# Latent attention heads: query columns of two heads in one product, rotary rows made once, blocks scaled at the end

## Chip, cores and metric

The kernel runs on one core of a Trainium2 chip. The metric is the time of one execution on the device in microseconds, as a median over runs; the engines are called PE (TensorE), DVE (VectorE), ACT (ScalarE), POOL (GpSimd), and SP is the queue that issues the DMAs.

## What is computed

Two decoder layers over 1024 rows of width 1024. The first layer's mixer is stick-breaking attention, the second's is latent attention; both layers have four memory heads and a SwiGLU. The change touches only the latent attention of the second layer, which has 12 heads, each with 64 plain and 32 rotary query columns:

```python
q = (_rms(c_q, mla_q_norm[j]) @ mla_w_q_up[j]).reshape(b, s, N_MLA_HEADS, MLA_QK)
kv = (_rms(c_kv, mla_kv_norm[j]) @ mla_w_kv_up[j]).reshape(b, s, N_MLA_HEADS, MLA_NOPE + MLA_V)
k = jnp.concatenate([kv[..., :MLA_NOPE], k_rope_h], axis=-1)
q = _rms(q, mla_g_qn[j])
k = _rms(k, mla_g_kn[j])
q = jnp.concatenate([q[..., :MLA_NOPE], _rope(q[..., MLA_NOPE:], positions)], -1)
k = jnp.concatenate([k[..., :MLA_NOPE], _rope(k[..., MLA_NOPE:], positions)], -1)
o = _causal_softmax_attn(q.transpose(0, 2, 1, 3), k.transpose(0, 2, 1, 3), v.transpose(0, 2, 1, 3))
```

## The kernel before

`latent_heads` works through the 12 heads as six pairs. Products in full precision are made of three matmuls each (`product3`, lines 84 to 86: high by high, low by high, high by low), so every operand is split into a high part (ACT copies it) and a low part (DVE or POOL subtracts).

**Preparing a pair.** The work is cut into units, and all units of a pair share one PSUM bank (`bank`, number 7), except in the opening, which has four. A unit waits until the one before it has left the bank (`free` and `released`). The units are: `kv 0` to `kv 3`, keys and values of 256 rows each, 12 matmuls of 256 columns; `q 0` to `q 3`, queries of one head and one half of the rows (`halves`: head 0 rows 0 to 511, head 0 rows 512 to 1023, then head 1), 18 matmuls of 512 columns each. The weights of a head are widened from 96 to 128 columns: the 32 rotary columns stand there a second time with their halves swapped, and one multiplication with `rope_table` does gain and rotation in one, because the scores sum over both copies. `ss` and `rq` (one each per head) sum the squares of the queries over the 96 columns by a matmul with `ones` and turn the sums with four transposes, `qnorm` makes the inverse root from them, and `kturn 0` to `kturn 3` turn the keys.

**Attention of a pair.** A pair has four jobs in the order of `halves`. A job has four score rows (128 queries each, against 128 to 512 keys in a half 0, against 640 to 1024 in a half 1), numbered 0 to 15 in the turn, and a softmax in the rows: DVE takes the maximum (line 1212) and multiplies it by the query's inverse root (line 1217), ACT takes the exponential and the row sum (line 1181), DVE takes the inverse of the sum (line 1226, step `I`) and multiplies the row by it (line 1232, step `R`). Then come 4 or 8 blocks of 128 keys, together 24 in a turn, numbered by `tau`: PE transposes a block (step `T`, line 1153), ACT copies it as the high part (line 1193), DVE subtracts the low part (line 1237), and two blocks later PE multiplies both with the values (step `V`, lines 1165 and 1167). `T` of a block waits for the low part of two blocks earlier. After the last block of a job, step `E` copies one half of the output bank (ACT, line 1199), adds the other (DVE, line 1243) and the block goes to DRAM. There is one output bank, so the first `V` of the next job waits for that addition.

**The order** is written out by hand. Turn `g` of a hardware loop runs the attention of pair `g` and between its blocks prepares pair `g + 1`: the dictionary `extras` says behind which `tau` a unit stands, and `plan` says how many score rows are made by the end of each `tau` (it runs 9 rows ahead into the next pair, so the rows 16 to 24 of a turn belong to the next pair). The list `OPENING` prepares pair 0. There are six turns; the last, here called the closing turn, prepares nothing. SP has one queue for the loads of weights and the stores of the output blocks. After the phase, `project_and_swiglu` begins.

## Time and profile before

| | |
|---|---|
| median of 3 runs | 2628.85 us (2626.62 to 2630.59) |
| the profiled execution | 2629.66 us, its span 2627.9 us |
| PE, DVE, ACT, POOL busy | 96%, 66%, 50%, 42% of the span |
| opening of the latent heads | 1482.5 to 1526.6 us, 44.1 us |
| turns 0 to 4 | 1526.6 to 1846.0 us, 319.4 us |
| closing turn | 1846.0 to 1884.3 us, 38.3 us |

The page gives each engine's busy time as a share of the span. The stretches of the latent heads come from the timeline: the opening begins with the first matmul of `kv 0`, and turn 0 with the first transpose of a block. A line can be that of a helper, so all products stand at lines 84 to 86; the tile names tell them apart.

### The profile page before, as it was taken

What the parts mean: (1) busy time and instruction counts of PE and PEld (TensorE: products, weight loads), DVE (VectorE), ACT (ScalarE), POOL (GpSimd) and SP (SyncE); (2) the same over time, 40 slices, a digit from 0 to 9 for tenths busy, and PEclk for the clock granted to TensorE, in tenths of its full rate; (3) what the DMA queues carried; (4) which work ended last, traced back from release to release, by engine and by line L of the source; (5) the groups of instructions that cost most, each with busy time, mean ns of one, the idle gap of its engine ahead of it and who ended that gap; (6) DMA issues with size and microseconds to landing.
All of it is one profiled execution on the core that took longest, in us unless ns stands there. A gap on an engine that the chain in (4) does not pass through costs nothing. (4 is left out here: it accounts for less than half of the span.)

```text
span 2627.9 us, 37382 instructions
## 1 busy us (share of the span) xinstructions
PE 2526.2 (96%) x12150; PEld 2057.7 (78%) x12150; DVE 1739.8 (66%) x2659; ACT 1310.6 (50%) x2483; POOL 1112.5 (42%) x839
## 2 busy tenths in 40 slices
PE   7999999999999999999989999999899999999999
PEld 6867777667888888888777777778687888888887
DVE  6767787855765666478655377777648665665595
ACT  6567777745433333444655366666545333333443
POOL 2134454311465566555411332332003665565554
PEclk9999999999999999999999999999899999999999
DMA  4111110153222232674302000000242322234843
GB/s 145 45 29 33 33 33 9 33 176 113 81 100 104 100 112 88 228 240 148 107 21 59 14 20 22 21 21 21 83 166 90 116 100 104 100 112 143 285 125 117
DMA packets 182796, 242.76 MB, mean 92 GB/s; under 512 B 31376, under 2 KB 105872, under 8 KB 182672
## 3 DMA queue, kind: packets, MB, share of 16 engines
q1 hardware_dynamic: 182672, 241.19, 27.7%
q8 instruction: 68, 1.11, 0.2%
q14 instruction: 56, 0.46, 0.1%
HBM read 175.60 MB, written 65.54 MB: 92 GB/s over the span
## 5 line engine op out<-in xcount | busy, mean ns | idle before, releaser
L2385 POOL TENSOR_TENSOR l0s_run_lo<-l0s_run,l0s_run_hi 128x512 fp32r<-128x512 f32 (+2 forms) x120 | 143.5, 1195 | 215.6 <-DVE l0s_run_hi L2538 215.6
L477 POOL TENSOR_TENSOR l1f_wd_lo<-l1f_d,l1f_wd_hi 128x512 fp32r<-128x512 f32 x77 | 108.0, 1403 | 104.6 <-ACT l1f_wd_hi L552 104.6
L477 POOL TENSOR_TENSOR l0f_wd_lo<-l0f_d,l0f_wd_hi 128x512 fp32r<-128x512 f32 x77 | 109.3, 1422 | 97.2 <-ACT l0f_wd_hi L552 97.0
L84 PE MATMUL banks<-l1f_T_hi,l1f_op_hi 128*128 128x512 f32 x352 | 137.1, 390 | 1.1 <-DVE l1f_T_lo L697 1.1
L84 PE MATMUL banks<-l0f_T_hi,l0f_op_hi 128*128 128x512 f32 x352 | 137.1, 390 | 1.0 <-DVE l0f_T_lo L697 1.0
L85 PE MATMUL banks<-l0f_T_lo,l0f_op_hi 128*128 128x512 f32 x352 | 137.0, 389 | 0.0
L85 PE MATMUL banks<-l1f_T_lo,l1f_op_hi 128*128 128x512 f32 x352 | 136.9, 389 | 0.0
L86 PE MATMUL banks<-l1f_T_hi,l1f_op_lo 128*128 128x512 f32 x352 | 136.9, 389 | 0.0
L86 PE MATMUL banks<-l0f_T_hi,l0f_op_lo 128*128 128x512 f32 x352 | 136.9, 389 | 0.0
L439 POOL TENSOR_TENSOR l1f_s<-l1f_raw 128x512 f32<-128x512 f32 x44 | 66.6, 1513 | 158.1 <-DMA l1f_raw<-in_w_ffn_gu_dram 135.3
L509 ACT ACTIVATE l1f_op_hi<-l1f_s 128x512 fp32r<-128x512 f32 x88 | 55.2, 631 | 140.4 <-PE banks L86 140.4
L509 ACT ACTIVATE l0f_op_hi<-l0f_s 128x512 fp32r<-128x512 f32 x88 | 55.2, 631 | 140.4 <-PE banks L86 140.4
L462 POOL TENSOR_TENSOR l1f_hid<-l1f_c,l1f_gate 128x512 f32<-128x512 f32 x44 | 67.5, 1535 | 129.6 <-DVE l1f_c L719 129.6
L462 POOL TENSOR_TENSOR l0f_hid<-l0f_c,l0f_gate 128x512 f32<-128x512 f32 x44 | 67.0, 1524 | 129.5 <-DVE l0f_c L719 129.5
L84 PE MATMUL banks<-ht_hi,l0s_w_hi 128*128 128x512 f32 x288 | 119.6, 415 | 1.4 <-DVE l0s_q L2033 1.2
L84 PE MATMUL banks<-l0f_wd_hi,l0f_a_hi 128*128 128x512 f32 x308 | 120.0, 390 | 0.6 <-DVE l0f_a_lo L760 0.6
L439 POOL TENSOR_TENSOR l0f_s<-l0f_raw 128x512 f32<-128x512 f32 x44 | 66.5, 1512 | 127.0 <-DMA l0f_raw<-in_w_ffn_gu_dram 102.9
L1237 DVE TENSOR_TENSOR l1aa_pt_lo<-banks,l1aa_pt_hi 128x512 fp32r<-128x512 f32 (+2 forms) x144 | 78.8, 554 | 62.3 <-ACT l1aa_pt_hi L1193 61.9
L86 PE MATMUL banks<-l0f_wd_hi,l0f_a_lo 128*128 128x512 f32 x308 | 119.8, 389 | 0.0
L85 PE MATMUL banks<-l0f_wd_lo,l0f_a_hi 128*128 128x512 f32 x308 | 119.8, 389 | 0.0
L84 PE MATMUL banks<-l1f_wd_hi,l1f_a_hi 128*128 128x512 f32 x308 | 119.8, 389 | 0.0
L85 PE MATMUL banks<-l1f_wd_lo,l1f_a_hi 128*128 128x512 f32 x308 | 119.8, 389 | 0.0
(536 smaller groups left out, 8456.1 us busy)
## 6 DMA issues: line engine op xcount, KB each, us to landing
l0f_raw<-in_w_ffn_gu_dram SPq DMA_DIRECT2D x22, 1024.0 KB, 5.0
l1f_raw<-in_w_ffn_gu_dram SPq DMA_DIRECT2D x22, 1024.0 KB, 4.9
l0f_a_raw<-hidden_rows SPq DMA_DIRECT2D x77, 256.0 KB, 3.9
l1f_a_raw<-hidden_rows SPq DMA_DIRECT2D x77, 256.0 KB, 3.4
...
```

The costliest lines, as they stand in the source:

```text
L84: pe.matmul(out, l_hi, r_hi, start=first, stop=False, skip_group_check=True)
L85: pe.matmul(out, l_hi, r_lo, start=False, stop=False, skip_group_check=True)
L86: return pe.matmul(out, l_lo, r_hi, start=False, stop=last, skip_group_check=True)
L439: pool.tensor_tensor(out[:], left, right, op).then_inc(s_made, 1)
L462: pool.tensor_tensor(hidden(q), cs[q][:], gate[q][:], ALU.mult).then_inc(hid_done, 1)
L477: pool.tensor_tensor(wd_lo[g % RING][:], held[HELD_AT[DOWN[p][1]]][i][:], as_f32(wd_hi[g % RING][:]), ALU.subtract).then_inc(wd_lo_done, 1)
L509: act.activation(op_hi[n][:], stationary(n, b), ACT.Copy).then_inc(op_hi_done, 1)
L1237: dve.tensor_tensor(self.pt_lo[tau % self.np][:, c0:HALF], self.t_ps[tau % 2][:, c0:HALF], as_f32(self.pt_hi[tau % self.np][:, c0:HALF]), ...
L2385: pool.tensor_tensor(run_lo[x % NR][:, f:HALF], run[x % NR][:, f:HALF], as_f32(run_hi[x % NR][:, f:HALF]), ALU.subtract).then_inc(run_spli ...
```

## The change

The four query units of a pair become two. `q 0` and `q 1` now make only the 64 plain columns, of both heads side by side in one 128 column product, for one half of the rows each, in two parts of nine matmuls. The rotary columns of all 12 heads are made in the opening, in three groups of four heads (`rope b half`, six units of 18 matmuls), multiplied by two tables spread over the partitions, stored in DRAM (`rope_dram`), and fetched for each pair by six DMAs into the lower half of `q32`. Squares are summed by matmuls with the squares as weights and two columns of ones (`twos`, or `fours` for the rotary groups, units `rss`), which need no turning afterwards; the rotary part of the sum goes through DRAM too (`base_dram`). The exponentials are no longer multiplied by the inverse row sum: step `R` is gone, step `I` takes four sums at once, and the inverse sums go to DRAM and come back spread over 64 partitions, where a second DVE operation in step `E` multiplies the output block by them. The order in `extras` and `plan` is new.

```diff
-    OPENING = ["kv 0", "kv 1", "kv 2", "kv 3", "q 0 0", "ksum 0", "q 0 1", "q 0 2", "knorm 0", "q 1 0", "q 1 1",
-               "wk", "ksum 1", "q 1 2", "kturn 0", "ss 0", "knorm 1", "rq 0", "qnorm 0", "S", "S", "q 2 0", "q 2 1",
-               "S", "kturn 1", "wq 0", "q 2 2", "q 3 0", "S", "S", "q 3 1", "S", "q 3 2", "S", "kturn 2", "ss 1",
-               "wq 1", "rq 1", "kturn 3", "S", "v0", "qnorm 1"]
-    extras = {0: ["q 0 0", "q 0 1"], 1: ["v1", "q 0 2"], 3: ["kv 0"], 4: ["kv 1"], 5: ["kv 2", "ksum 0"],
-              6: ["kv 3", "knorm 0", "wk"], 7: ["q 1 0", "ksum 1", "q 1 1", "q 1 2", "knorm 1"], 8: ["ss 0"],
-              9: ["rq 0"], 10: ["kturn 0"], 11: ["kturn 1"], 12: ["qnorm 0", "q 2 0", "wq 0"], 13: ["q 2 1", "v0"], 15: ["q 2 2"],
-              16: ["q 3 0"], 17: ["q 3 1", "q 3 2"], 18: ["wq 1", "kturn 2"], 19: ["ss 1"],
-              20: ["rq 1", "qnorm 1"], 21: ["kturn 3"]}
-    plan = [9, 9, 9, 9, 10, 10, 11, 12, 12, 12, 13, 14, 15, 16, 17, 18, 18, 20, 20, 21, 22, 22, 23, 24, 25]
+    OPENING = ["kv 0", "kv 1", "kv 2", "kv 3", "wr 1", "rope 0 0", "ksum 0", "rope 0 1", "knorm 0", "rss 0 0", "q 0 0", "ksum 1",
+               "rss 0 1", "q 0 1", "knorm 1", "ss 0", "kturn 0", "q 1 0", "rq 0", "q 1 1", "qhi 0", "qnorm 0", "kturn 1", "ss 1",
+               "wr 2", "rope 1 0", "S", "qhi 1", "rq 1", "S", "qnorm 1", "S", "rope 1 1", "S", "rss 1 0", "kturn 2", "S", "qhi 2",
+               "rss 1 1", "S", "kturn 3", "S", "qhi 3", "S", "S", "rope 2 0", "wq", "wk", "rope 2 1", "rss 2 0", "v0", "rss 2 1"]
+    extras = {1: ["v1"], 2: ["kv 0"], 3: ["kv 1"], 4: ["kv 2", "ksum 0"], 5: ["kv 3", "knorm 0"], 6: ["q 0 0", "ksum 1", "wk"],
+              7: ["q 0 1", "knorm 1"], 8: ["ss 0", "rq 0"], 9: ["qhi 0"], 10: ["kturn 0", "qnorm 0"], 11: ["kturn 1"], 12: ["q 1 0"],
+              13: ["q 1 1", "v0"], 14: ["ss 1", "rq 1", "qhi 1"], 15: ["qhi 2", "wq"], 16: ["kturn 2", "qnorm 1"], 17: ["qhi 3"],
+              18: ["kturn 3"]}
+    plan = [9, 9, 9, 9, 10, 11, 12, 13, 13, 14, 15, 16, 16, 17, 18, 18, 19, 20, 20, 21, 22, 22, 23, 24, 25]
...
             elif kind == "I":
-                s = 4 * step[0] + step[1]
-                one = slice(s % 4, s % 4 + 1)
-                dve.wait_ge(self.exp_done, turn * self.ns + s + 1)
-                dve.reciprocal(self.rinv[:, one], self.rsum[:, one]).then_inc(self.inv_done, 1)
-            elif kind == "R":
...
-                dve.tensor_scalar(row[:], row[:], self.rinv[:, one], None, ALU.mult).then_inc(self.rows_done, 1)
+                n = step[0]
+                dve.wait_ge(self.exp_done, turn * self.ns + 4 * n + 4)
...
+                dve.reciprocal(self.rinv[n % 2][:], self.rsum[n % 2][:]).then_inc(self.inv_done, 1)
...
             elif kind == "E":
                 n = step[0]
                 dve.wait_ge(self.tmp_done, turn * self.nj + n + 1)
+                dve.tensor_tensor(self.o_sum, self.o_ps[n % len(self.o_ps)][0:HD, :], self.o_tmp, ALU.add).then_inc(self.out_done, 1)
+                dve.wait_ge(self.out_done, 1 + turn * self.nj + n + 1)
                 dve.wait_ge(self.stored[n % 2], 16 + 16 * (turn * (self.nj // 2) + n // 2))
-                dve.tensor_tensor(self.o_out[n % 2][:], self.o_ps[n % len(self.o_ps)][0:HD, :], self.o_tmp[:],
-                                  ALU.add).then_inc(self.out_done, 1)
+                dve.wait_ge(self.scale_in[n % 2], 16 * (turn * (self.nj // 2) + n // 2 + 1))
+                dve.tensor_tensor(self.o_out[n % 2], self.o_sum, self.o_scale[n % 2], ALU.mult).then_inc(self.out_scaled, 1)
...
+    def store_scale(self, sp, n, turn=0):
+        sp.wait_ge(self.inv_done, turn * self.nj + n + 1)
+        with self.nc.allow_non_contiguous_dma("row scales"):
+            sp.dma_start(self.scale_dram[n % self.nj].rearrange("(i p) -> p i", p=P), self.rinv[n % 2][:]).then_inc(self.scale_stored[n % 2], 16)
...
+                elif kind == "rope":
+                    b, half = int(n[0]), int(n[1])
+                    if half == 0:
+                        pe.wait_ge(wr_lo, b + 1)
+                    free(what, g)
+                    for c in range(NQ):
+                        last = product3(pe, bank_of(what, g)[:], wr["hi"][b % 2][:, c, :], wr["lo"][b % 2][:, c, :],
+                                        cq["hi"][:, c, columns(half)], cq["lo"][:, c, columns(half)], c == 0, c == NQ - 1)
+                    last.then_inc(rope_made, 1)
...
                 elif kind == "ss":
-                    h = int(n[0])
...
-                    for half in range(2):
-                        last = pe.matmul(bank_of(what, g)[half * HD:(half + 1) * HD, :], ones[:], q_sq[half][:],
+                    half = int(n[0])
                     free(what, g)
+                    pe.wait_ge(q_squared, 2 * g + half + 1)
+                    for i in range(HT):
+                        last = pe.matmul(bank_of(what, g)[:, 2 * i:2 * i + 2], q_sq[half][:, i * P:(i + 1) * P], twos[:],
                                          start=True, stop=True, skip_group_check=True)
```

The first place is on PE, at the start of a turn of the loop: the blocks tau 0 to 2, whose transposes read `l1aa_p` and whose products read `l1a_v`. Before, from the end of the first two parts of `q 0`:

```order
L84 MATMUL banks<-cq_hi,l1a_wq_hi_14507 128x512
L85 MATMUL banks<-cq_lo,l1a_wq_hi_14507 128x512
L86 MATMUL banks<-cq_hi,l1a_wq_lo_14509 128x512
L1153 MATMUL banks<-ident,l1aa_p_1_14536 128x128
L1153 MATMUL banks<-ident,l1aa_p_2_14537 128x128
L1153 MATMUL banks<-ident,l1aa_p_3_14538 128x128
L1165 MATMUL banks<-l1aa_pt_hi_14553,l1a_v 128x128
L1167 MATMUL banks<-l1aa_pt_lo_14556,l1a_v 128x128
L84 MATMUL banks<-cq_hi,l1a_wq_hi_14507 128x512
L85 MATMUL banks<-cq_lo,l1a_wq_hi_14507 128x512
L86 MATMUL banks<-cq_hi,l1a_wq_lo_14509 128x512
```

And in the change, from the transposes of tau 1 to the first product of the next job:

```order
L1142 MATMUL banks<-ident,l1aa_p_1_14535 128x128
L1142 MATMUL banks<-ident,l1aa_p_2_14536 128x128
L1142 MATMUL banks<-ident,l1aa_p_3_14537 128x128
L1154 MATMUL banks<-l1aa_pt_hi_14552,l1a_v 128x128
L1156 MATMUL banks<-l1aa_pt_lo_14555,l1a_v 128x128
L1140 REGISTER_ALU
L1142 MATMUL banks<-ident,l1aa_p_2_14536 128x128
L1142 MATMUL banks<-ident,l1aa_p_3_14537 128x128
L1150 ISA
L3530 ISA
L1154 MATMUL banks<-l1aa_pt_hi_14550,l1a_v 128x512
L1156 MATMUL banks<-l1aa_pt_lo_14553,l1a_v 128x512
```

The 18 matmuls of a query unit, 12 behind tau 0 and 6 behind tau 1, stand there no longer; the transposes of tau 2 follow the product of tau 1 directly.

The second place is on DVE, around the end of job 2 (tau 16 and 17). Before, from the maximum of a score row to the addition of the output block and what follows it:

```order
L1226 RECIPROCAL l1aa_rinv<-l1aa_rsum 128x1
L1232 TENSOR_SCALAR l1aa_p_1_14536<-l1aa_p_1_14536,l1aa_rinv 128x256
L1209 REGISTER_ALU
L1212 TENSOR_REDUCE l1aa_raw_nmx<-banks 128x1
L1217 TENSOR_TENSOR l1aa_nmx<-l1aa_raw_nmx,l1a_rq 128x1
L1236 REGISTER_ALU
L1237 TENSOR_TENSOR l1aa_pt_lo_14556<-banks,l1aa_pt_hi_14553 128x512
L1241 REGISTER_ALU
L1242 ISA
L1243 TENSOR_TENSOR l1aa_o_out_14562<-banks,l1aa_o_tmp 64x512
```

And in the change (`l1aa_parts` is the sum before scaling):

```order
L1203 TENSOR_REDUCE l1aa_raw_nmx<-banks 128x1
L1208 TENSOR_TENSOR l1aa_nmx<-l1aa_raw_nmx,l1a_rq 128x1
L3403 REGISTER_ALU
L3407 SCALAR_TENSOR_TENSOR l1a_kt_lo<-banks,l1a_gcol,l1a_kt_hi 128x512
L3333 TENSOR_TENSOR l1a_q_a<-l1a_q_y 128x8
L3335 SCALAR_TENSOR_TENSOR l1a_q_b<-l1a_q_a,l1a_q_dev 128x8
L3336 REGISTER_ALU
L3337 SCALAR_TENSOR_TENSOR l1a_rq<-l1a_q_b,l1a_q_y 128x8
L1222 REGISTER_ALU
L1223 TENSOR_TENSOR l1aa_pt_lo_14555<-banks,l1aa_pt_hi_14552 128x512
L1228 TENSOR_TENSOR l1aa_parts<-banks,l1aa_parts 64x512
```

The low part of `kturn 2` and the three operations of `qnorm 1` have moved ahead of the last low part and of the addition that frees the output bank; the scaling of rows is gone.

## Rows read from the trace of the kernel before

**Rows 1.** Windows: one turn (turn 2) and the closing turn.
```profile
core 0: us, PE busy (x) PEld busy (x) DVE busy (x) ACT busy (x) POOL busy (x), PEclk, DMA share, GB/s
1606.15:1670.00 63.85, 60.37 (x361) 50.43 (x360) 50.09 (x121) 42.01 (x100) 18.19 (x19) 1.00 0.08 22
1846.00:1884.30 38.30, 31.49 (x153) 25.89 (x154) 26.66 (x59) 20.65 (x43) 1.27 (x1) 0.78 0.18 55
```
**Rows 2.** Waits of PE in one turn: us in total, times, longest.
```profile
PE banks L3347 <- DVE l1a_kt_lo L3268: 1.0, 1, 1.0
...
PE banks L1165 <- DVE l1aa_o_out L1243: 0.5, 2, 0.3
```
**Rows 3.** Timeline of PE: a query unit, its 4th and last matmul, then `ss`.
```profile
1543.60 0.39 PE L84 MATMUL banks<-cq_hi,l1a_wq_hi 128*128 128x512 f32 x1
...
1546.79 0.40 PE L86 MATMUL banks<-cq_hi,l1a_wq_lo 128*128 128x512 f32 x1
...
1548.79 1.08 PE L3347 MATMUL banks<-l1a_q_sq,l1a_ones 128*64 128x512 f32 x4 [0.70 <-ACT l1a_q_sq L3161]
1549.80 0.55 PE L1153 MATMUL banks<-ident,l1aa_p 128*128 128x128 f32 x3
...
1551.74 0.62 PE L3355 MATMUL banks<-ident,l1a_q_sq 128*128 128x128 f32 x4
1552.19 0.38 PE L1153 MATMUL banks<-ident,l1aa_p 128*128 128x128 f32 x2
```
**Rows 4.** Timeline of PE: sums with two columns, phase before.
```profile
1479.11 1.95 PE L2923 MATMUL banks<-l1i_ones,l1i_q_sum 128*128 128x2 f32 x16 [0.84 <-POOL l1i_q_sum L2750]
```
**Rows 5.** Waits of PE in the opening.
```profile
PE banks L3355 <- ACT l1a_q_sq L3167: 2.5, 2, 1.8
PE banks L3347 <- ACT l1a_q_sq L3161: 1.6, 2, 1.1
```
**Rows 6.** Timeline of PE, start of turn 2, with query parts between.
```profile
1650.09 0.22 PE L2984 MATMUL banks<-causal,ident_r 128*128 128x128 f32 x1
...
1658.19 0.49 PE L1165 MATMUL banks<-l1aa_pt_hi,l1a_v 128*128 128x512 f32 x1 [0.30 <-DVE l1aa_o_out L1243]
```
**Rows 7.** Timeline of PE, start of the closing turn, nothing between.
```profile
1841.33 0.22 PE L2984 MATMUL banks<-causal,ident_r 128*128 128x128 f32 x1
...
1847.78 0.66 PE L1153 MATMUL banks<-ident,l1aa_p 128*128 128x128 f32 x2 [2.79 <-DVE l1aa_pt_lo L1237]
1848.79 0.77 PE L1165 MATMUL banks<-l1aa_pt_hi,l1a_v 128*128 128x512 f32 x1 [0.35 <-issue]
```
**Rows 8.** Timeline of DVE, same place.
```profile
1846.10 0.93 DVE L1232 TENSOR_SCALAR l1aa_p<-l1aa_p,l1aa_rinv 128x1024 f32<-128x1024 f32 x2
1846.94 1.15 DVE L1237 TENSOR_TENSOR l1aa_pt_lo<-banks,l1aa_pt_hi 128x512 fp32r<-128x512 f32 x2
1848.01 0.67 DVE L1243 TENSOR_TENSOR l1aa_o_out<-banks,l1aa_o_tmp 64x512 f32<-64x512 f32 x1
```
**Rows 9.** Windows: granted clock behind that start (columns as in rows 1).
```profile
1848.00:1850.00 2.00, 1.65 (x6) 0.98 (x6) 1.11 (x3) 0.38 (x1) 1.27 (x1) 0.50 0.07 17
...
1854.00:1856.00 2.00, 1.38 (x10) 1.17 (x10) 1.60 (x3) 1.55 (x3) 0.00 (x0) 0.97 0.68 267
...
1528.00:1530.00 2.00, 0.48 (x3) 0.05 (x1) 2.00 (x3) 0.38 (x1) 2.00 (x2) 1.00 0.00 0
```
**Rows 10.** Timeline of PE: `kturn 0` and `kturn 1`, one score row between.
```profile
1617.51 0.62 PE L3364 MATMUL banks<-ident,l1a_k 128*128 128x128 f32 x4
...
1620.44 0.63 PE L3364 MATMUL banks<-ident,l1a_k 128*128 128x128 f32 x4 [0.55 <-DVE l1a_kt_lo L3268]
```
**Rows 11.** Groups by line, whole program: count, busy us, mean ns.
```profile
L1232 DVE TENSOR_SCALAR l1aa_p<-l1aa_p,l1aa_rinv 128x128 f32<-128x128 f32 (+3 forms) x96 | 53.8, 565 | 2.3
...
L3268 DVE SCALAR_TENSOR_TENSOR l1a_kt_lo<-banks,l1a_gcol,l1a_kt_hi 128x512 fp32r<-128x512 f32 x24 | 17.9, 745 | 4.9 <-ACT l1a_kt_hi L3176 4.9
...
L1226 DVE RECIPROCAL l1aa_rinv<-l1aa_rsum 128x1 f32<-128x1 f32 x96 | 14.7, 153 | 3.3 <-ACT l1aa_p L1181 3.3
```

More of the change, by code:

```diff
@@ L1064, in __init__ @@
                           for j in range(blocks_of(half))]
-        steps, made, exps, inverses, rows = [], 0, 0, 0, 0
+        steps, made, exps = [], 0, 0
         def score_up_to(count):
@@ L1070, in score_up_to @@
                 exp_up_to(made)
-                row_up_to(made - 1)
                 steps.append(("S", made // 4, made % 4))
                 made += 1
+                if made % 4 == 1 and made > 4:
+                    steps.append(("I", made // 4 - 1))
         def exp_up_to(count):
@@ L1112, in __init__ @@
             steps += rest
-        row_up_to(plan[-1])
+        exp_up_to(plan[-1])
         self.steps = steps
         self.first_steps = [s for s in steps if s[0] not in "VE" or s[1] >= 0]
-        self.closing = [s for s in steps if s[0] not in "SPIR" or s[1] < self.nj] + (rest if wrap else [])
+        self.closing = [s for s in steps if s[0] not in "SPI" or s[1] < self.nj] + (rest if wrap else [])
     def product(self, tau):
@@ new lines, in load_base, with store_rotary, spread_table @@
+            def load_base(g):
+                sp.dma_start(base[:].rearrange("p a h i -> p (a h i)"), base_dram[:, bass.ds(g * G, G)]).then_inc(base_in, 16)
+            def store_rotary(r):
+                b, half = ROPES[r]
+                sp.wait_ge(rope_copied, r + 1)
+                for kind in range(2):
+                    sp.dma_start(rope_dram[kind, b * P:(b + 1) * P, columns(half)], rope_out[kind][r % 2][:]).then_inc(rope_stored[r % 2], 16)
+            def spread_table():
+                for n in range(4):
+                    for kind, row, first, count in ((0, HD, 0, ROPE), (1, HD + ROPE + H, 0, H), (1, HD + ROPE, H, H)):
+                        at_row = n * ROPE + first
+                        sp.dma_start(tables[kind][at_row:at_row + count, :], table[row:row + count, :]).then_inc(spread, 16)
@@ L3155, in prepare @@
                     u = int(n[0])
                     h, half = halves[u]
[L3157 to L3167 removed]
+                    act.wait_ge(rope_in[h], 48 * (g + 1))
@@ L3168, in prepare @@
+                    act.wait_ge(q_scaled[h], 2 * g + half + 1)
+                    act.activation(qt["hi"][:, h, columns(half)], q32[:, h, columns(half)], ACT.Copy).then_inc(q_hi, 1)
                 elif kind == "ksum":
@@ L3271, in ready @@
             def ready(dve, h, half, g):
-                dve.wait_ge(q_scale, 2 * g + h + 1)
+                dve.wait_ge(q_scale, 2 * g + half + 1)
             dve.memset(gcol[:], 1.0).then_inc(made_ones, 1)
-            dve.memset(ones[0:QK, :], 1.0)
-            dve.memset(ones[QK:P, :], 0.0).then_inc(made_ones, 1)
+            for h in range(2):
+                dve.memset(twos[h * HD:(h + 1) * HD, h:h + 1], 1.0)
+                dve.memset(twos[h * HD:(h + 1) * HD, 1 - h:2 - h], 0.0)
+            for i in range(4):
+                for j in range(4):
+                    last = dve.memset(fours[i * ROPE:(i + 1) * ROPE, j:j + 1], 1.0 if i == j else 0.0)
+            last.then_inc(made_ones, 1)
             at_.dve(dve, opening, 0, lambda dve, what, g: prepare(dve, what, 0), ready)
@@ L3319, in prepare @@
                         pe.wait_ge(wk_lo, g + 1)
+                        if isinstance(g, int) and g == 1:
+                            for s in range(2):
+                                pe.wait_ge(rope_stored[s], 96)
                     free(what, g)
@@ L3326, in prepare @@
                     last.then_inc(kv_made, 1)
+                elif kind == "rope":
+                    b, half = int(n[0]), int(n[1])
+                    if half == 0:
[5 more added lines that the diff above has]
+                    last.then_inc(rope_made, 1)
+                elif kind == "rss":
+                    r = 2 * int(n[0]) + int(n[1])
+                    if r == 0:
+                        pe.wait_ge(made_ones, 2)
+                    free(what, g)
+                    pe.wait_ge(rope_squared, r + 1)
+                    for i in range(HT):
+                        last = pe.matmul(bank_of(what, g)[:, 4 * i:4 * i + 4], q_sq[r % 2][:, i * P:(i + 1) * P], fours[:],
+                                         start=True, stop=True, skip_group_check=True)
+                    last.then_inc(rss_made, 1)
```

418 lines of the change are left out of this document (261 added, 157 removed).

## The prediction

> **What bounds the kernel now.** I read the windows first, cut at the borders of the phase [rows 1]. In turn 2 PE is busy 60.4 of 63.85 us at the full clock, against 50.1 for DVE, 42.0 for ACT and 18.2 for POOL. So PE bounds the turn, and what a change takes from its instructions comes back only as far as no other chain is laid bare. Next I read what PE waits for in that turn: five entries, 1.0 the longest and 0.5 the shortest [rows 2], in all 3.3 us; nearly every chain of DVE and ACT is covered. The closing turn shows the same attention without cover: PE has 31.5 us of work in 38.3, at 0.78 of the clock [rows 1]. It is the only sample of what a turn does when PE runs out of work, and it is my measure for the new one. Then I read the places where a turn is thinnest, its start and the turns of keys, and price them one by one.
>
> **PE, per turn.** From the fourth matmul of a query unit at 1543.60 to its eighteenth at 1546.79 [rows 3] there are 14 steps: 3.19 / 14 = 0.228 us each. Seventy-two matmuls become 36: 36 x 0.228 = **-8.2**. A head's `ss` holds PE for 1.01 (1548.79 to 1549.80) and its turning for 0.45 (1551.74 to 1552.19) [rows 3], together 1.46. The new `ss` of a half is eight products with two columns; sixteen such took 1.95 [rows 4], so 0.97 for eight. Two of them: **-1.0**. PE alone would give 63.85 - 9.2 = 54.7 us a turn.
>
> **DVE, ACT, POOL, SP, per turn.** DVE loses 16 row scalings of 565 ns and 12 of 16 inverses of 153 ns [rows 11]: -9.0 and -1.8. Four further multiplications of 64x512, by the addition of the same shape at 0.67 [rows 8], give +2.7. That is no term of the sum, since DVE doesn't bound; it shortens chains where a scaling lies in them. The scales go to DRAM and back while the next job's blocks are made. The trace has no such trip of 512 elements. From below it costs nothing, since the block is free (the addition comes first, and frees the bank) and only the multiplication waits; from above, a multiplication that waits holds everything behind it on DVE, and a job is never shorter than a fifth of a turn, about 12 us. I take nothing for the turns, and leave it as a mishap within the upper range.
>
> **Where a turn loses its cover.** Four places.
>
> First, its start. Now 18 query matmuls stand between the last score row and the first product of the next job; from 1650.09 to 1658.19 it is 8.1 us [rows 6], with PE waiting only 0.30 at the end. In the closing turn the query matmuls are missing: from 1841.33 to 1848.79 it is 7.5 us, of which PE waits 2.79 and 0.35 [rows 7]. The change makes every turn start so. One thing shortens it: of the DVE work in between, the scalings of 0.93 for two [rows 8] and one before them are gone, 1.5 us, so that I put the stretch at 6.0. PE has 2.3 us in it (its listed records; `kv 0` stands only at tau 2, behind the product that waits). Gap 3.6.
>
> Second, `kturn 0` and `kturn 1`. They share the one bank; start to start it is 2.93 with 0.55 waiting and a score row of 1.25 between [rows 10]. The new plan puts no row between, so the chain of copying out (PE's four transposes, ACT's high part, DVE's low part of 0.745 [rows 11]) shows: 0.55 + 1.25 less what shorter DVE queues give, 1.6. `q 1 0` behind them waits for the same bank, 0.8.
>
> Third, tau 16 to 18. The order shows DVE doing `kt_lo` (0.745) and the three operations of `qnorm 1` (the smallest ones take about 0.15 each [rows 11]) ahead of the last low part and the addition (0.67 [rows 8]) that frees the output bank. With a maximum and the low part ahead, of some 0.85 and 0.6, that is 3.8 us between two products between which PE has about 0.6 of work: gap 3.2.
>
> Fourth, `ss` and single rows, 0.4.
>
> Sum 9.6 in place of 3.3. The turn is 63.85 - 9.2 - 3.3 + 9.6 = **61.0** at the full clock.
>
> **The clock.** Behind the uncovered start of the closing turn the granted clock stands at 0.50 (1.2 GHz), from 1848 to 1854, and is back at 0.97 in the window from 1854 [rows 9]: 6 us at half speed, where PE has work for 3 at full, so 3 us lost. Behind a gap of 1.9 us at the start of turn 0 it stayed at 1.00 (last row of [rows 9]). So from below the price is nothing, from above 3 us for each start; two of the new gaps (3.6 and 3.2) are larger than the one that let it fall, but what follows is partly waiting anyway, which a slower PE fills. I take half, 1.6: the turn is **62.6**, and five turns are 5 x -1.25 = **-6.2**.
>
> **The opening.** Six rotary units of 18 matmuls come (108), 36 of the query's go: 72 x 0.228 = +16.4. Six `rss` by 0.97 are +5.8, and the changed `ss` -1.0. Of the waits of now, 2.5 stand at the turning of sums, which falls away, and 1.6 at the products of squares [rows 5]. New ones: ACT, which widens the rotary weights (`wr 1`) when their DMA has landed, holds `ksum` and the squares behind it; POOL's low parts of the queries come behind `wr 2`; single rows wait for them. I have no row for this; from below nothing, from above 7, an earlier start of everything after late weights. I take 3.5, near the 4.1 of now. +16.4 + 5.8 - 1.0 - 4.1 + 3.5 = **+20.5**, from 17 to 24.
>
> By the Trainium skill ("TensorE: Matmul & The Clock Gate", section "Back-to-back issue gap") a sustained stream of N=512 matmuls is spaced about 131 ns apart. The rows show 228 [rows 3], so this chip doesn't do that here; by the page's figure, an estimate, removing 36 from a turn gives only 4.7 us and adding 72 to the opening costs 9.4, and the kernel would end 17.5 - 7.0, some 10 us, later than by the row's spacing (36 x 0.097 less given back in each of five turns, 72 x 0.097 less added in the opening). It speaks against the change, and the rows overrule it.
>
> **The closing turn.** The same chains without `R`: -1.5 at the start, where the clock fell too, and the last score rows follow each other faster, each by a scaling of about 0.9. From nothing to -8; I take **-4**.
>
> **Sum.** The profiled execution took 2629.66 us, 0.8 above the median. 2628.85 + 20.5 - 6.2 - 4 = **2639 us**.
>
> **The rivals.**
> A (0.40): as summed, gaps of 8 to 11 us a turn with one fall of the clock. 2639; a turn from 61.4 to 64 gives 2633 to 2650.
> B (0.18): the same gaps, and the clock holds, as after the gap of 1.9 us. The turn is 61.0: 5 x -2.85 = -14.3, and 2629. Within 0.2%.
> C (0.29): the chains shrink more than I allow. DVE loses 8 of its 50 us a turn, and each maximum, low part and addition stands behind less; the stretch of the start falls to 5, `kt_lo` is hidden by ACT's and PE's own order. Gaps of 6 us, no fall of the clock: 63.85 - 9.2 - 3.3 + 6 = 57.4, five times -6.5 = -32, closing -6: 2628.85 + 20.5 - 32 - 6 = 2611. For it speaks that PE has 9.2 us less to do in each of five turns and only 21 more in the opening. Against it, that the closing turn, with little else to do, still left PE waiting 7 of 38 us. It decides from gaps of under 8.5 us a turn.
> D (0.13): the turn loses its clock twice (start and tau 17), 3 us each, and is as long as now or longer, 64.5: +3; or the rotary weights land late and the opening takes +27. 2628.85 + 20.5 + 3 - 2 + 6 is 2656.
>
> **How the numbers follow.** What a measurement of this kernel can tell from no change is about 0.2%, 5 us. The single forecast is A's, 2639, with 2633 to 2650 as its own range. The range of 2608 to 2653 takes in most of C and D's lower half. Faster by more than 0.2% (below 2623.6): C and a tail of B, 0.31. Within: B and the lowest of A, 0.19. Slower: A and D, 0.50.
>
> **What would show it.** Opening 64 to 65 us, with 72 matmuls more. Turns of 61 to 63 (57 for C, 64.5 for D); PE busy 51 of them at full clock; a wait of 2 to 4 us for a low part or the output bank at each turn's start, and one of about 3 us near tau 17; the clock row below 10 at the starts of all turns. DVE busy some 42 a turn. The multiplication of step `E` shows no wait for a scale except in the last job; if it waits in the turns, my zero for the round trip is the step that failed. If PE's waits in a turn come to less than 7 us, the start was mis-sized; if the opening is longer than 68, the rotary weights or ACT's order.

## The result, and where the time went

The changed kernel takes 2675.31 us (median of 4 runs, 2668.14 to 2676.43) against 2629.39 for the kernel before: a ratio of 1.0163, 95% interval 1.0149 to 1.0177. It is slower by some 43 us by that ratio (45.9 between the two medians), where I forecast 10 and ended my range at 2653.

The head of the page after; the spans are 2672.6 and, before, 2627.9 us:

```profile
span 2672.6 us, 37394 instructions
PE 2523.3 (94%) x12090; PEld 2065.3 (77%) x12090; DVE 1709.4 (64%) x2545; ACT 1303.7 (49%) x2445; POOL 1107.5 (41%) x812
...
PEclk9999999999999999999999999899899999999999
```

Windows of the changed kernel: the opening, turns 0, 2 and 3, the closing turn. From here on I cut at the first product of the first job whose output waits for the bank, since that row is easily found in every kernel; so the opening is longer by 2.4 to 4 us than in the forecast's cut, and the closing turn shorter.

```profile
core 0: us, PE busy (x) PEld busy (x) DVE busy (x) ACT busy (x) POOL busy (x), PEclk, DMA share, GB/s
1482.00:1555.80 73.80, 64.28 (x330) 54.31 (x330) 28.11 (x85) 29.65 (x63) 22.39 (x18) 0.92 0.35 92
1555.80:1622.48 66.68, 55.36 (x327) 48.44 (x325) 43.33 (x94) 40.23 (x93) 16.42 (x15) 0.93 0.15 30
1690.51:1758.64 68.13, 56.73 (x324) 49.26 (x325) 44.44 (x94) 40.01 (x92) 16.34 (x15) 0.90 0.16 36
1758.64:1824.09 65.45, 53.17 (x324) 45.96 (x325) 44.34 (x94) 39.81 (x92) 16.16 (x15) 0.97 0.16 35
1891.37:1923.96 32.59, 27.32 (x150) 22.10 (x151) 23.55 (x45) 18.19 (x38) 0.87 (x1) 0.90 0.31 70
```

And the kernel before, cut in the same way (opening, turn 2, closing turn):

```profile
1482.52:1530.55 48.03, 41.97 (x227) 34.86 (x228) 27.38 (x66) 27.07 (x66) 23.14 (x25) 0.97 0.14 36
1658.19:1722.03 63.84, 60.41 (x360) 50.49 (x361) 50.16 (x121) 42.20 (x99) 18.20 (x20) 1.00 0.08 22
1848.79:1884.19 35.40, 30.72 (x150) 25.46 (x151) 24.00 (x53) 18.36 (x39) 0.55 (x1) 0.78 0.19 60
```

So the account is: opening +25.8 (73.80 against 48.03); five turns +17.3 (1555.80 to 1891.37 is 335.57, against 1530.55 to 1848.79, 318.24); closing turn -2.8; from the last product to the next phase +5.0 (12.9 against 7.9); and the opening began 0.5 earlier. Together 44.8, the difference of the spans. What the reader is to see in the rows: the turn did lose its 36 matmuls (360 records to 324) and 5.7 us of DVE, and yet got longer, at a granted clock of 0.90 to 0.97. Length less busy time is what PE stands idle: 3.4 us in turn 2 before, 11.4 after.

The waits of PE in turn 2 (they answer to [rows 2]):

```profile
PE banks L1154 <- DVE l1aa_parts L1228: 4.5, 2, 3.7
PE banks L1142 <- DVE l1aa_pt_lo L1223: 2.4, 2, 1.9
PE banks L3525 <- DVE l1a_kt_lo L3407: 2.1, 1, 2.1
PE banks L84 <- ACT l1aa_p L1172: 1.1, 2, 1.0
PE banks L3515 <- DVE l1a_q L3382: 1.1, 2, 0.8
PE banks L84 <- DVE l1a_kt_lo L3407: 0.2, 1, 0.2
```

They are 11.4 us, where 3.1 to 3.3 stood before. The places are those of the forecast: 1.9 and 0.8 at the start of a turn, 2.1 between the two turns of keys, 3.7 for the output bank. The timeline of DVE ahead of this last one shows the very order that the change wrote:

```profile
1735.91 0.69 DVE L1223 TENSOR_TENSOR l1aa_pt_lo<-banks,l1aa_pt_hi 128x512 fp32r<-128x512 f32 x1 [0.55 <-ACT l1aa_pt_hi L1184]
1736.52 0.68 DVE L1203 TENSOR_REDUCE l1aa_raw_nmx<-banks 128x1 f32<-128x512 f32 x1
1737.23 1.13 DVE L1208 TENSOR_TENSOR l1aa_nmx<-l1aa_raw_nmx,l1a_rq 128x1 f32<-128x1 f32 x1
1738.29 0.74 DVE L3407 SCALAR_TENSOR_TENSOR l1a_kt_lo<-banks,l1a_gcol,l1a_kt_hi 128x512 fp32r<-128x512 f32 x1
...
1739.44 0.69 DVE L1223 TENSOR_TENSOR l1aa_pt_lo<-banks,l1aa_pt_hi 128x512 fp32r<-128x512 f32 x1
1740.16 0.68 DVE L1228 TENSOR_TENSOR l1aa_parts<-banks,l1aa_parts 64x512 f32<-64x512 f32 x1
```

Behind each of the three (the start, the second turn of keys, the output bank) the granted clock may fall: turns 0, 1, 2 and 4 have three stretches at half clock, turn 3 has one. Windows of turn 2: behind the wait for the second turn of keys, and behind the wait for the output bank:

```profile
1721.00:1723.00 2.00, 1.72 (x14) 1.75 (x14) 0.97 (x6) 1.64 (x4) 0.00 (x0) 0.87 0.00 0
1723.00:1725.00 2.00, 1.85 (x6) 1.37 (x6) 1.50 (x5) 0.13 (x1) 0.00 (x0) 0.50 0.00 0
...
1739.00:1741.00 2.00, 0.01 (x1) 0.04 (x1) 1.74 (x6) 1.27 (x4) 1.14 (x1) 0.64 0.00 0
1741.00:1743.00 2.00, 2.00 (x5) 1.61 (x6) 1.38 (x2) 0.00 (x0) 0.13 (x1) 0.50 0.00 0
1743.00:1745.00 2.00, 2.00 (x11) 1.90 (x10) 0.75 (x1) 0.00 (x0) 0.00 (x0) 0.50 0.00 0
```

### The profile page after: what moved, and what is told of

Same layout as the page of the kernel before. It is cut to its first block and busy times, and to the rows that moved or that the text cites. A ratio compares the mean times of both kernels' runs of the same rounds, so it can differ in the third digit from the quotient of the medians.

```text
span 2672.6 us, 37394 instructions
## 1 busy us (share of the span) xinstructions
PE 2523.3 (94%) x12090; PEld 2065.3 (77%) x12090; DVE 1709.4 (64%) x2545; ACT 1303.7 (49%) x2445; POOL 1107.5 (41%) x812
## 5 line engine op out<-in xcount | busy, mean ns | idle before, releaser
L86 PE MATMUL banks<-l1f_wd_hi,l1f_a_lo 128*128 128x512 f32 x308 | 119.8, 389 | 0.0
```

The lines of the kernel that those rows point to most:

```text
L86: return pe.matmul(out, l_lo, r_hi, start=False, stop=last, skip_group_check=True)
```

## The experiments

Two theories stood at the start. **Single holes:** the turn is PE's work plus a few places where a chain is laid bare, each with its own price and its own fall of the clock; mend the places and the gain comes. **A floor:** a chain over the other engines is hardly shorter than PE's work was, and freed PE time turns into waiting wherever the units are put. Turns are compared from one such first product to the next; a "spell" is a stretch at half clock, some 3.5 us long (sometimes 7). The waits and the windows are those of one profiled execution for each run, of its turn 2 where nothing else is said.

### Mending the places of the changed kernel

**The keys later.** An edit of the order alone:

```diff
...
-              16: ["kturn 2", "qnorm 1"], 17: ["qhi 3"],
-              18: ["kturn 3"]}
+              17: ["qhi 3", "kturn 2", "qnorm 1"],
+              19: ["kturn 3"]}
```

> The changed kernel with kturn 2 and qnorm 1 one block later (behind tau 17 and so behind the addition that frees the output bank) and kturn 3 behind tau 19. Theory 1 (a hole on PE costs its length and then the time at half clock behind it): the wait of 3.7 us for the output bank at tau 18 falls below 1 and the clock does not fall there; a turn loses some 2.9 us of waiting and 2.8 of slow clock, five turns 28 us, so the time is near 1.006 of the kernel before in place of 1.016. Theory 2 (the half clock costs nothing of its own, since what follows waits anyway): only the waiting comes back, 14 us, 1.011. Theory 3 (DVE is simply late, the wait moves to another place): 1.016 as now.

Measured: 2674.96 us, ratio 1.0165 (1.0142 to 1.0187), the same as the change. The wait for the output bank fell from 3.7 to 2.5 us, not below 1, and a turn's waits from 11.4 to 10.5; its spells stayed (0.89 in turn 2). The mend took away a third of the hole and nothing of the time, as theory 3 said.

**Query matmuls back at the start of the turn.**

```diff
-    extras = {1: ["v1"], ...  6: ["q 0 0", "ksum 1", "wk"], 7: ["q 0 1", "knorm 1"],
+    extras = {0: ["q 0 0"], 1: ["v1", "q 0 1"], ...  6: ["ksum 1", "wk"], 7: ["knorm 1"],
```

> The changed kernel with the query unit q 0 0 and q 0 1 (18 matmuls) behind tau 0 and tau 1, where the query matmuls stood before the change, in place of tau 6 and 7. Theory 1: the waits of 1.9 and 0.8 us at the start of a turn vanish and with them the fall of the clock there (1.7 us); holes of 1 to 2 us open at tau 6 to 8, where the matmuls are missing; net 3 us a turn, 15 us, about 1.010 to 1.012 of the kernel before. Theory 3 (the same time is waited elsewhere, as the chain over DVE and ACT is the bound): 1.016.

Measured: 2681.96 us, 1.0184 (1.0150 to 1.0219), no gain; its interval takes in that of the change. The 3.7 us for the output bank stayed, the waits at the start shrank, and among others these stand in their place (before the move 1.1 us for an exponential, and none for `l1a_q` at line 84):

```profile
PE banks L84 <- ACT l1aa_p L1172: 2.1, 2, 2.0
PE banks L84 <- DVE l1a_q L3382: 1.7, 1, 1.7
```

All waits of the turn sum to 12.9 us, against 11.4. The holes moved.

**A start filled with matmuls that compute nothing.**

```diff
+              ... 18: ["kturn 3"], 23: ["fill"]}
+                elif kind == "fill":
+                    released("kturn 3", g)
+                    for i in range(20):
+                        pe.matmul(bank[:, 0:2 * P], k["ident_r"][:], k["strict"][:], start=True, stop=True, ...)
```

> The changed kernel with 20 matmuls of 256 columns that compute nothing (into the free bank of the units, constants as operands) at the end of a turn, in front of the wait at the start of the next. They do no useful work and take away no wait of the chain, so this prices the clock alone. Theory 1: the granted clock stays at 1.00 over the start of the turns, and each of five turns is about 1.7 us shorter: 8 us in all, about 1.013 of the kernel before. Theory 2 (the half clock behind the start is hidden by waiting anyway): no gain, 1.016, or a loss of up to 0.5 us a turn where the fill outlasts the wait.

Measured: 2685.22 us, 1.0205 (1.0178 to 1.0231), slower than the change. The fill took 2.4 us where 1.9 were idle, and two waits of 0.75 and 0.82 us stood behind it; at the start of turn 3 the clock still fell to 0.50. As a price for the clock it is inconclusive, since the start was not filled to its end. Theory 1 of its expectation fell.

**The last scales first** in SP's queue:

```diff
-            load_passage(sp, passage, w_out, ot_dram, passage_in)
             at_.step(sp, 3, PAIRS - 1)
+            load_passage(sp, passage, w_out, ot_dram, passage_in)
```

> The changed kernel with the store and load of the last job's row scales issued ahead of the four large loads of the next phase in the closing turn. Theory 1 (the store of the scales, 14 us, stood behind and beside 1.5 MB of loads): the last multiplication waits less than 1 us in place of 6.2, the gap before the next phase falls from 8.2 us to 3 or 4, and the time falls by 4 to 5 us, to about 1.0145. Theory 2 (the two way trip itself takes 14 us wherever it stands, or the later loads hold the next phase instead): no change within 1 us.

Measured: 2677.81 us, 1.0185 (1.0161 to 1.0209), no gain. SP's queue in the changed kernel, and then in this one:

```profile
1913.97 0.58 SPq L1246 DMA_DIRECT2D row_scales<-l1aa_rinv  x1
...
1928.83 0.45 SPq L1250 DMA_DIRECT2D l1aa_out_scale<-row_scales  x1
```
```profile
1909.19 0.59 SPq L1246 DMA_DIRECT2D row_scales<-l1aa_rinv  x1
...
1920.11 0.45 SPq L1250 DMA_DIRECT2D l1aa_out_scale<-row_scales  x1
1920.60 0.80 SPq L135 DMA_DIRECT2D l1f_w_raw<-in_w_out_dram  x1
```

The load of the scales waits for their store, 14.9 us beside the large loads and 10.9 without them. The last multiplication waited 2.35 us in place of 6.22, but now the loads of the next phase were issued 1.4 us behind the last product (1919.23), where they had been issued 12.1 ahead of it, and the stretch to the next phase stayed at 12.9. Theory 2 held: the trip's length must be paid in front of one or the other.

**POOL's split of the weights elsewhere.** The diff moves `wq` from behind tau 15 to behind tau 18 on ACT, and behind `qlo 3` in POOL's own order (`POOL_ORDER`, not shown):

```diff
-    15: ["qhi 2", "wq"], ... 18: ["kturn 3"]}
+    15: ["qhi 2"], ...       18: ["kturn 3", "wq"]}
```

> The changed kernel with the weight split of the next queries (ACT copy, POOL subtraction of 1.81 us) behind kturn 3 at tau 18 in place of tau 15. In the changed kernel the DVE multiplication of a row maximum took 1.13 us in place of 0.16 and ended with that POOL subtraction, in the chain before the 3.7 us wait for the output bank. If POOL's work holds the multiplication, it takes 0.2 to 0.4 here, the wait falls to 2.7 or less, and the kernel gains 1 us a turn: 5 us, 1.014 to 1.015 (more only if a fall of the clock goes too). If it is a matter of records only, nothing changes.

Measured: 2665.52 us, 1.0134 (1.0112 to 1.0156), 8 us or so better than the change; the two intervals just overlap, and the five turns of its profile are 7.5 us shorter (328.1 against 335.6). The multiplication of the maximum in the same place took 0.16 in place of 1.13, the wait for the output bank is 2.8 in place of 3.7, and a turn's waits are 10.3:

```profile
1727.67 0.68 DVE L1203 TENSOR_REDUCE l1aa_raw_nmx<-banks 128x1 f32<-128x512 f32 x1
1728.38 0.16 DVE L1208 TENSOR_TENSOR l1aa_nmx<-l1aa_raw_nmx,l1a_rq 128x1 f32<-128x1 f32 x1
```

**All of it.** The moves above together, with `kturn 1` two blocks behind `kturn 0` and two score rows of the opening between rotary units; and the same with `wq` at tau 19.

> The changed kernel with all moves together: q 0 0 and q 0 1 behind tau 0 and 1 with the key units one block later, kturn 1 two blocks behind kturn 0, kturn 2 and qnorm 1 behind the addition of the output block, the last scales ahead of the next phase's loads, and two score rows of the opening between rotary units. Each move alone has shifted waits more than removed them. If the waits are those of single places, each with its fall of the clock, all together leave 5 us of waits a turn, turns of 59 to 61 us and 1.000 to 1.006; if they are the length of the chain, 10 us of waits remain and it is 1.012 or more.

> All moves together (which took 1.011 of the kernel before) with the weight split at tau 19. By the same reasoning the wait of 2.6 us for the output bank falls to 1.5 and the turn by 1 us, 1.009; if both falls of the clock in a turn (7 us each at half) shrink to one, 1.004. Below 1.000 only if the turn comes under 59 us, which no experiment has shown.

Measured: 2657.66 us, 1.0111 (1.0094 to 1.0128), and 2660.25, 1.0112 (1.0095 to 1.0129). That is a third of the loss of the kernel taken back, between what the two theories of the first expectation said; the move of `wq`, worth 8 us by itself, added nothing here. By parts it is clearer. The five turns together took 319.75 and 319.67 us (mean 63.9), against 335.57 in the change and 318.24 before: the moves gave back 15.8 of the 17.3 us that the turns had lost, and not more. (Turns 0 to 3 took 64.1 to 64.9 us against 63.6 to 64.0 before, turn 4 took 60.8 and 61.3 against 62.9.) The openings stayed at 74.2 and 74.4 us (the spreading of score rows brought nothing), 26 us above the kernel before, and that is nearly all that is left of the loss.

Turn 2 of the two runs, the first with two spells of 7 us, the second with one of 3.5:

```profile
1686.08:1751.01 64.93, 56.19 (x327) 48.56 (x326) 46.92 (x95) 40.10 (x92) 16.40 (x15) 0.89 0.17 35
```
```profile
1688.96:1753.21 64.25, 53.00 (x325) 45.74 (x325) 47.70 (x95) 39.69 (x92) 16.52 (x15) 0.97 0.16 36
```

PE was busy 3.2 us less in the second and waited 2.8 more (11.5 against 8.7): what PE gained at the full clock it spent waiting, and the turn was no shorter than before the change with 36 matmuls more. So single places explain why the turns got longer. They don't explain why the turns never got shorter than before; for that the question became what PE's time is worth at all.

### What PE's time is worth in the kernel before

Now only the number of matmuls in the query units of the turns was changed, in the kernel before, at their places: 36 fewer (every second chunk left out), 24 and 12 fewer, 12 more.

```diff
                     for c in range(*PARTS[part]):
+                        if c % 2 and not (isinstance(g, int) and g == 0):
+                            continue
...
```

> The kernel before, where the query units of the turns (not of the opening) leave out every second chunk of their sum: 36 of the 72 query matmuls of a turn are missing, as in the change, and nothing else moves or is added (the queries are then wrong sums, and only the time counts). Theory A (PE bounds the turn as its 95% busy says): the turn goes from 63.85 to near 55.7 us, 41 us less in all, 0.984 of the kernel before. Theory B (the chain of score row, maximum, exponential and the single banks is hardly shorter than PE's work, so that freed time turns into waits and the clock falls in them): the turn stays over 61 us, and the kernel at 0.995 or above.

> The kernel before with three more 512 column matmuls in each query unit of the turns (the first chunk is made twice): 12 matmuls, 2.7 us, more a turn, nothing else. If PE sets the turn from above, as the missing 36 did not show from below, each turn grows by 2.7 us: 13.7 us in all, 1.005 of the kernel before. If a chain over the other engines already sets it, PE's waits (3.1 us a turn) take up the 2.7 and the ratio is 1.000 to 1.002.

> The kernel before with one of six chunks left out of the query units of the turns: 12 matmuls, 2.7 us, less a turn (the queries are then wrong sums, and only the time counts). With 12 more a turn took 65.9 us, as it is 63.9, with 36 fewer 65.4. If the turn has a floor from the other engines near 61 to 62 us and the loss at 36 fewer is the clock's, this small cut still gains: 62 to 63 us a turn, without falls of the clock, 0.997 to 0.999. If the kernel before already stands on the floor, the turn stays at 63.9 or grows, 1.000 or more.

> As the last, with two of six chunks left out: 24 matmuls, 5.5 us, less a turn. Floor near 61 to 62 us: waits of 6 to 7 us a turn, one fall of the clock a turn, and 62 to 64 us a turn, 0.998 to 1.001. Kernel before already on the floor: over 64.5, 1.002 or more.

Windows of one turn each: 12 more; 12 fewer; 24 fewer (turns 2 and 3); 36 fewer.

```profile
1662.39:1728.26 65.87, 62.72 (x373) 52.63 (x373) 50.72 (x121) 42.13 (x99) 18.18 (x20) 1.00 0.08 21
```
```profile
1661.38:1725.18 63.80, 57.98 (x348) 48.16 (x349) 50.13 (x121) 42.09 (x99) 18.17 (x20) 1.00 0.08 22
```
```profile
1660.19:1724.00 63.81, 55.17 (x336) 45.91 (x337) 50.15 (x121) 42.07 (x99) 18.20 (x20) 1.00 0.08 22
1724.00:1789.38 65.38, 56.76 (x337) 46.87 (x337) 50.07 (x121) 42.19 (x99) 18.18 (x20) 0.97 0.08 21
```
```profile
1723.74:1789.21 65.47, 55.79 (x324) 46.14 (x325) 50.13 (x121) 42.18 (x99) 18.13 (x20) 0.95 0.08 21
```

| matmuls in a turn's query units | PE's waits in that turn | turn at clock 1.00 | ratio to the kernel before |
|---|---|---|---|
| 12 more | 3.1 | 65.87 | 1.0042 (1.0024 to 1.0059) |
| as before | 3.1 | 63.84 | 1 |
| 12 fewer | 5.7 | 63.80 | 0.9998 (0.9986 to 1.0009) |
| 24 fewer | 8.6 | 63.81 | 1.0029 (1.0016 to 1.0042) |
| 36 fewer | 9.5 | none; 65.47 at 0.95 | 1.0045 (1.0029 to 1.0062) |

This is the main result. Upward PE sets the turn: 12 matmuls more cost 2.0 us of their 2.7. Downward nothing is gained: 12 fewer give 2.6 us more waiting, 24 fewer 5.5, within 0.1 us what was taken out (12 x 0.228 = 2.7, 24 x 0.228 = 5.5), and a turn at the full clock stands at 63.8. With 12 fewer every turn is within 0.2 us of the same turn before; with 24 fewer turn 2 alone shows it, since the others have spells (64.5 to 66.2). The kernel before stood on that floor with PE just covering it. The new waits lie in several places. Turn 2 with 24 fewer, and the same places in the kernel before:

```profile
PE banks L1165 <- DVE l1aa_o_out L1243: 3.7, 3, 1.5
PE banks L3349 <- ACT l1a_q_sq L3161: 2.0, 1, 2.0
PE banks L1153 <- DVE l1aa_pt_lo L1237: 0.8, 1, 0.8
```
```profile
PE banks L1165 <- DVE l1aa_o_out L1243: 0.3, 1, 0.3
PE banks L3347 <- ACT l1a_q_sq L3161: 0.7, 1, 0.7
```

The output bank, the squares of ACT and the last low part are what PE had been covering.

The two turns of the run with 24 fewer also give a price of the clock: the same instructions, 8.6 and 8.5 us of waits, one spell of 3.5 us between 18 and 22 us into the turn in the one and none in the other, 65.38 against 63.81: 1.57 us for that spell. With 36 fewer a third spell cost 1.4 to 1.5 (turn 2 with three took 66.91, turns 1 and 3 with two 65.41 and 65.47). It isn't a constant: in the two turns of "all of it" above, whose kernels differ in the place of `wq` alone, 10 us more at half clock stand beside 0.7 us more of length and 2.8 less of waiting.

With 36 fewer the floor isn't shown. Of the 8.2 us taken out, 6.4 turned into waits and some 3.6 into work at half clock. At 1.57 each, the turn without its two spells would take 62.3 us, under 63.8; no turn of that run is without them.

The same cut in the changed kernel, 18 of its 36 matmuls:

> The changed kernel with the same cut: 18 of the 36 query matmuls of a turn are left out (their sums are then wrong, and only the time counts), nothing moves. If PE still set the turn it would lose 4.1 us, 20 us in all, 1.009 of the kernel before. Theory B: the turn is bound by the chain of rows and banks, and it stays within 1 us of 67 us, the kernel at 1.013 to 1.018.

Measured: 2671.20 us, 1.0149 (1.0123 to 1.0176). Its turns took 64.3 to 68.2 us, 66.2 on average against 67.1: 0.9 of 4.1 us came back. That is what theory B said, but not for its reason. The waits didn't grow (11.4 us a turn on average, as in the change); it is the time at half clock that grew, from 10.8 to 17.7 us a turn. Its turn 2 had 13.7 us at half clock, as turn 2 of the change:

```profile
1688.03:1752.57 64.54, 53.19 (x307) 46.84 (x307) 43.63 (x94) 40.16 (x92) 16.31 (x15) 0.89 0.15 35
```

Against the 68.13 there, 3.6 of the 4.1 us came back. So a floor of 63.8 us isn't shown for the changed kernel with its own order; what holds its turns up is its waits and its clock.

### The other parts

**Scaling of the output block alone**, in the kernel before: `R` taken out, one `I` for four rows, the sums through DRAM, the second operation in `E`; units and order as before.

> The kernel before with one part of the change alone: the exponentials are not scaled, the inverse row sums go through DRAM and scale the output block; query units, rotary columns and the order of the units are those of before. DVE loses 9 us a turn. Theory A (PE bound): the turns stay at 63.4 to 63.9, the closing turn gains 2 to 3, the end of the phase is 3 to 5 longer for the scale trip: 0.999 to 1.001. Theory B (the chain over DVE is close behind PE): the same in the turns, as PE's waits were 3 us only; at most 2 us a turn. If it is over 1.005, the scale trip or its place in SP's queue costs in the turns too, which I had at nothing.

Measured: 2640.42 us, 1.0057 (1.0036 to 1.0078): slower. Windows of its turn 2:

```profile
1657.81:1723.36 65.55, 60.62 (x360) 50.50 (x361) 47.38 (x96) 41.71 (x99) 17.93 (x20) 1.00 0.14 29
```

At the full clock and with PE's work unchanged the turn is 1.7 us longer, its waits 4.7 in place of 3.1, and DVE is busy 47.4 where my sum (50.1 - 9.0 - 1.8 + 2.7) says 42.0. The multiplication took 0.85 us on average where the addition took 0.68, and that of the maximum 0.34 in place of 0.26. The closing turn took 38.4 us in place of 35.4. Which of the moved operations lengthens the turns was not tried.

**The opening with a sixth of the rotary products:**

```diff
-                    for c in range(NQ):
+                    for c in range(1):
```

> The changed kernel with one of six chunks in the six rotary units of the opening (the rotary sums are then wrong, and only the time counts): 90 matmuls of 0.228 us, 20.5 us, are left out. If the opening is bound by PE, as my sum took it, it falls from 73.8 to 53 or 54 us and the kernel to 1.008; if the chain behind the units (square, two tables, store, load, split) is as long, the opening stays above 60.

Measured: 2665.66 us, 1.0149 (1.0123 to 1.0175). Its opening:

```profile
1478.08:1546.60 68.52, 51.19 (x240) 44.24 (x240) 29.28 (x85) 29.52 (x63) 22.11 (x18) 0.72 0.38 99
```

Ninety matmuls, 20.5 us, left out bring 5.3. PE waits 18.8 us, of them 6.6 for the first squares (ACT, in the changed kernel, stood 6.6 us until the rotary weights had landed) and 4.0 for POOL's low part of the queries, and the clock is at 0.72. Of the 20.5 us, 5.3 came back, 7.8 became waits (18.8 against 11.0) and some 7.4 went to the slower clock (PE is busy 51.2 where 64.3 - 20.5 is 43.8). So most of what PE gives up in the opening is lost too, about half of that to the chain and half to the clock.

**Whose floor is it?** The run with 36 fewer again, with step `R` cut to 32 columns:

```diff
-                dve.tensor_scalar(row[:], row[:], self.rinv[:, one], None, ALU.mult)...
+                dve.tensor_scalar(row[:, 0:ROPE], row[:, 0:ROPE], self.rinv[:, one], None, ALU.mult)...
```

> The kernel before with 36 query matmuls fewer a turn (which took 65.4 us a turn, 9.5 of it waits of PE) and the scaling of the exponentials cut to their first 32 columns, so that DVE has some 6 us less a turn (most of the row is then not scaled, and only the time counts). If the floor of 63.8 us is the work of DVE, the turn falls by 4 to 6 us, to 60 or less; if it is a chain in which the scaling hardly stands, as the run with the scaling taken out of the kernel before hints, it stays within 1.5 us of 65.4.

Measured: 2618.91 us, 0.9956 (0.9942 to 0.9970), against 1.0045 with the whole rows scaled. Its five turns took 62.5 us on average against 65.6, for 3.9 us less of DVE in a turn (46.2 busy against 50.1). A part of the 3 us is the clock: its turns 1 and 3 have one spell (62.4 us), those of the other run two (65.4). Where it had more time at half clock than the other run, 10.2 us against 6.8, its turn 2 still took 63.6 against 65.5, 1.9 us less. It lies between what the two theories said. The scaling stands in the chain for a good part, but this run leaves its work out and doesn't replace it by anything; ACT's part, and another order of the units in the kernel before, were not tried.

## Why the prediction was wrong

The direction was right, and so was the form of the likeliest case, A: work of PE, plus waits, plus clock, plus a longer opening. The size was off four times over, and the range ended 22 us short of the result. My sum gave +10.3 us; the trace has +44.8. Of the 34.5 between them 23.5 lie in the five turns, 5.3 in the opening, 5.0 behind the last product and 1.2 in the closing turn (and -0.5 ahead of the opening).

**The turn** is the step that failed: "So PE bounds the turn, and what a change takes from its instructions comes back only as far as no other chain is laid bare", and with it 62.6 us a turn. Measured, on average of five turns, it is 67.1:

| us a turn | forecast | measured |
|---|---|---|
| PE's work at the full clock | 51.4 (63.85 - 9.2 - 3.3) | 51.5 (turn 3: 53.17 less half of its 3.5 us spell) |
| waits | 9.6 | 11.4 |
| clock | 1.6 | 4.2 (the rest) |

PE's work was right. The waits were 1.8 short and the clock 2.6, and I gave back hole by hole what is lost together: in the kernel before, with nothing added or moved, the same 36 matmuls taken out made a turn 1.6 us longer (65.47 against 63.84), 6.4 us in waits and 3.6 in the clock against 8.2 of work. At 12 and 24 matmuls the work came back as waits to within 0.1 us. So 95% busy and 3.3 us of waits didn't mean that PE's time could be had: what the turn needs besides PE was already as long. In the changed kernel its order added the rest: with the units moved, the turns went back to 63.9. Which of the other engines and banks make up that length was tried for DVE's scaling alone.

The other terms:

- **The holes** were placed rightly, all four. Sizes: start 2.7 (forecast 3.6); keys 2.1 and 0.2 to 0.5 (1.6 and 0.8); output bank 3.7 (3.2), of which 1.0 was POOL's hold on DVE, which I had not in the sum; sums and rows 2.2, with a wait of 1.0 for an exponential among them (0.4).
- **The clock** was mis-sized: one fall of 1.6 us a turn. A spell can cost 1.6, but four of the five turns have three, and in three of those the third lasts 7 us. Turn 2, with two spells more than turn 3 and the third longer, took 68.13 against 65.45: PE was 3.6 us longer at work and 0.9 less idle. And the row that I read as the clock behind the gap of turn 0 (the last of [rows 9]) ends at 1530.00, inside that gap; the clock did stay at 1.00 behind it.
- **The opening** was +25.8 against +20.5. PE's busy time grew by 22.3 (forecast 21.2; the clock stood at 0.92 against 0.97), and the waits by 3.5 (11.0 against 7.5) where I let them shrink by 0.6. To the first transposes of a block it is 71.4 us, past the 68 that I had named as the sign of late rotary weights or ACT's order; ACT did stand 6.6 us for those weights. The 1526.6 at which I ended the opening before is the second block; its first transposes stand at 1523.4.
- **The closing turn**: -2.8 against -4, within its bounds.
- **The scale trip**: next to nothing in the turns of the changed kernel, as forecast (the multiplication waited 0.7 us once); but it didn't hide for the last job, where the multiplication waited 6.2 us and the next phase began 5.0 later. I named the last job as an exception and put no price on it.
- Rival C, "the chains shrink more than I allow" (0.29), did not come. Less work on DVE can shorten the turn (the run with `R` cut), but what the change put in `R`'s place took that back: with the scaling alone the turn was 1.7 us longer. B (0.18) lacks the spells. D, 2656 with two falls a turn, was nearest. A's upper end was mis-added as well: a turn of 64 us gives 2646 by the sum, not 2650.
- The spacing of 131 ns that the Trainium skill states ("TensorE: Matmul & The Clock Gate", section "Back-to-back issue gap") is not seen in the changed kernel either: eight steps in the last rotary unit took 1.81 us, 0.226 each. It would have moved the sum towards the result for a reason that isn't the cause.

## What to carry to other kernels

An engine that is busy 95% of a loop's time need not be what bounds it from below. Before counting removed work as gain, leave out a slice of it in place (12 matmuls a turn sufficed) and see whether the turn moves; here the idle time grew by what was left out, within 0.1 us. When it doesn't move, look at the clock too before calling it a floor: with 36 left out, and in the changed kernel, a good part of the time went into half clock and not into waiting. On PE a covered chain that is laid bare can cost more than its wait: up to 1.6 us for each spell of some 3.5 us behind it, and less where the turn waits anyway. Work that is made once, ahead of a loop, is paid in full there even if the loop gives nothing back.

## What was new about the chip

- **A small DVE operation is held by POOL.** The multiplication of a maximum (one column, all operands in SBUF) took 1.13 us where it takes 0.16, and ended at 1670.32 in turn 1, when POOL's subtraction `wq_lo` ended:

```profile
1669.19 1.13 DVE L1208 TENSOR_TENSOR l1aa_nmx<-l1aa_raw_nmx,l1a_rq 128x1 f32<-128x1 f32 x1
```
```profile
1668.50 1.81 POOL L3164 TENSOR_TENSOR l1a_wq_lo<-l1a_wq_raw,l1a_wq_hi 128x768 fp32r<-128x768 f32 x1
```

With POOL's work elsewhere it took 0.16 (above). The Trainium skill ("GPSIMD Engine Reference", section "1. Specifications") says that the two engines share their SBUF interface and contend where a DVE instruction has two SBUF inputs. The trace agrees: this multiplication has two, and took 1.13 us beside POOL's subtraction.
- **The same waits don't always bring a spell.** At the start of turn 3 PE idled 1.91 and 0.82 us and the clock stayed at 1.00; at the start of turn 2 the same two waits (1.90 and 0.82) were followed by a spell:

```profile
1757.00:1759.00 2.00, 0.80 (x4) 0.52 (x5) 1.72 (x4) 1.50 (x3) 0.80 (x1) 1.00 0.94 191
1759.00:1761.00 2.00, 2.00 (x17) 1.96 (x16) 1.46 (x2) 0.10 (x1) 0.48 (x1) 1.00 0.22 7
...
1690.00:1692.00 2.00, 1.50 (x10) 1.41 (x11) 1.72 (x3) 0.38 (x1) 1.28 (x1) 0.94 0.66 180
1692.00:1694.00 2.00, 2.00 (x10) 2.00 (x10) 0.35 (x1) 0.62 (x3) 0.00 (x0) 0.50 0.50 83
```

- **512 row sums stored four bytes at a time** take long for their 2 KB: from the issue of the store to that of the load which needs it, it was 9 to 11.5 us in the turns, 10.9 for the last job with its loads behind it and 14.9 beside 1.5 MB of loads.
